# Low rotary score passes of two heads, moved behind all others and cut to 64 rows each

## The reference, cut to what matters

```python
q_rope = apply_rope(q_rope, cos, sin)          # 16 heads, 64 wide
k_rope = apply_rope(k_rope, cos, sin)          # 64 wide, one for all heads
q = concatenate([q_nope, q_rope])              # 128 + 64
k = concatenate([k_nope, k_rope])
s = q @ k.T * scale                            # for each head, causal, blocks of 128 queries
o = softmax(s) @ v
```

## Time and profile before

| | |
|---|---|
| median of 3 runs | 1814.77 us (1813.79 to 1815.86) |
| profiled execution, span from first to last instruction | 1812.8 us |
| profiled execution, own time beside the span | none is given |
| TensorE busy | 1792.2 us, 99%, mean granted clock 0.998 |
| VectorE busy | 1501.2 us, 83% |
| ScalarE busy | 918.5 us, 51% |
| GpSimd busy | 181.3 us, 10% |
| attention, 8 pairs of heads | from 129.6 us, first score matmuls 31.8 us apart |

### The profile page before, as it was taken

The page is one execution under the profiler, slowest core; times in us unless marked ns, Lnnn a source line. Parts: engine busy times, 40 slices in busy tenths (PEclk is TensorE's granted clock), DMA queues, the critical chain, the costliest instruction groups (busy, mean ns, idle before and its releaser), DMA issues.

```text
span 1812.8 us, 28067 instructions
## 1 busy us (share of the span) xinstructions
PE 1792.2 (99%) x10892; PEld 1609.5 (89%) x10892; DVE 1501.2 (83%) x1837; ACT 918.5 (51%) x1163; POOL 181.3 (10%) x100
## 2 busy tenths in 40 slices
PE   9999999999999999999999999999999999999997
PEld 7888989978879999999999999988888888888886
DVE  4167677799989988888888888889888999989986
ACT  5357666544356656655665566543433334333442
POOL 2353323000020000000000000000011111100003
PEclk9999999999999999999999999999999999999999
DMA  6232433598124654565456545778375474754832
GB/s 235 82 105 91 131 119 129 201 360 303 71 106 174 232 209 174 185 214 209 174 184 214 211 174 181 252 299 334 148 281 197 178 286 162 272 202 162 306 123 93
DMA packets 131731, 351.73 MB, mean 194 GB/s; under 512 B 7632, under 2 KB 80208, under 8 KB 113232
## 3 DMA queue, kind: packets, MB, share of 16 engines
q1 hardware_dynamic: 57264, 275.67, 40.7%
q10 hardware_dynamic: 74400, 75.26, 12.6%
HBM read 268.59 MB, written 82.31 MB: 194 GB/s over the span
## 4 chain that ended last, share of the span: by engine, by line
PE 95%; DVE 3%; issue 1%; ACT 1%; DMA 0%; ACTq 0%; DVEq 0%
PE bank L2121 31%; PE bank L2125 31%; PE bank L2126 31%; PE bank L2291 1%; PE bank L2283 0%; PE bank L2281 0%; DVE w_lo L1497 0%; DMA first_raw<-weights 0%; DVE small L1607 0%; DVE up_lo L1703 0%; DVE small L1452 0%; DVE pt_lo L1470 0%; ACT rows L1153 0%; DVE norm_t L1695 0%; DVE rows L1676 0%
## 5 line engine op out<-in xcount | busy, mean ns | idle before, releaser
L2121 PE MATMUL bank<-up_hi,w_hi 128*128 128x256 f32 x1808 | 512.0, 283 | 1.1 <-issue 0.9
L2125 PE MATMUL bank<-up_lo,w_hi 128*128 128x256 f32 x1808 | 511.7, 283 | 0.0
L2126 PE MATMUL bank<-up_hi,w_lo 128*128 128x256 f32 x1808 | 511.6, 283 | 0.0
L2121 PEld LDWEIGHTS bank<-up_hi,w_hi 128*128 128x128 f32 x1808 | 347.1, 192 | 1.8 <-issue 1.6
L2125 PEld LDWEIGHTS bank<-up_lo,w_hi 128*128 128x128 f32 x1808 | 347.1, 192 | 0.0
L2126 PEld LDWEIGHTS bank<-up_hi,w_lo 128*128 128x128 f32 x1808 | 347.1, 192 | 0.0
L1212 ACT ACTIVATE w_hi<-d_b 128x1024 fp32r<-128x1024 f32 x180 | 189.5, 1061 | 299.5 <-PE bank L2126 243.2
L2121 PE MATMUL bank<-w_hi,down_act 128*128 128x512 f32 x864 | 336.6, 390 | 0.0
L2125 PE MATMUL bank<-w_lo,down_act 128*128 128x512 f32 x864 | 336.2, 389 | 0.0
L2126 PE MATMUL bank<-w_hi,down_act 128*128 128x512 f32 x864 | 336.2, 389 | 0.0
L1000 ACT ACTIVATE w_hi<-up_b 128x1024 fp32r<-128x1024 f32 x180 | 186.9, 1054 | 157.9 <-PE bank L2126 126.7
(11 more groups left out here) (214 smaller groups left out, 2931.8 us busy)
## 6 DMA issues: line engine op xcount, KB each, us to landing
up_b<-up_weights SPq DMA_DIRECT2D x128, 512.0 KB, 5.0
d_b<-down_weights SPq DMA_DIRECT2D x64, 1024.0 KB, 5.1
down_act<-acts_kept SPq DMA_DIRECT2D x56, 1024.0 KB, 4.9
acts_kept<-h_hi ACTq DMA_DIRECT2D x32, 896.0 KB, 5.9
acts_kept<-h_lo ACTq DMA_DIRECT2D x32, 896.0 KB, 6.8
raw<-weights SPq DMA_DIRECT2D x46, 512.0 KB, 3.2
o_b<-out_weights SPq DMA_DIRECT2D x16, 1024.0 KB, 7.6
o_act<-o_kept SPq DMA_DIRECT2D x13, 1024.0 KB, 9.3
```

Of the source, the lines that this page charges most:

```text
L2121: first_pass = pe.matmul(out_, a_hi, b_hi, start=start, stop=False, skip_group_check=more)
L2125: pe.matmul(out_, a_hi, b_lo, start=False, stop=False, skip_group_check=more)
L2126: return pe.matmul(out_, a_lo, b_hi, start=False, stop=stop, skip_group_check=more)
```

## The change

The low rotary pass is taken out of `scores` and done for both heads in a new function `score_lows`, called after the scores of both heads. It takes the 64 rows with the high part of the query only, head 0's in rows 0 to 63 and head 1's in rows 64 to 127 (`tile_position` 0 and 64), block by block, the heads alternating. `kr_lo` becomes one tile without zeros. `scored` is now raised twice, by the last two matmuls of `score_lows`. Since block 0 stays open while block 2 of the same bank begins, block 2 no longer starts with the flag that clears.

```diff
-        kr_hi, kr_lo = sb("kr_hi", [P, S], f32r), sb("kr_lo", [P, 2, S], f32r)
-        place[0] += 2 * KB
+        kr_hi, kr_lo = sb("kr_hi", [P, S], f32r), sb("kr_lo", [P, S], f32r)
+        place[0] += 4 * KB
...
-            for h in range(2):
-                last = dve.memset(kr_lo[64 - 64 * h:128 - 64 * h, h, :].bitcast(f32), 0.0)
-            last.then_inc(zeroed, 1)
...
             def key_rope_lo():
                 dve.wait_ge(rope_hi, 1)
-                dve.wait_ge(zeroed, 1)
-                for half, h in zip(halves, range(2)):
-                    last = dve.tensor_tensor(kr_lo[half, h, :], rot[half, :], kr_hi[half, :].bitcast(f32), ALU.subtract)
-                last.then_inc(rope_split, 1)
+                dve.tensor_tensor(kr_lo[:, :], rot[:, :], kr_hi[:, :].bitcast(f32), ALU.subtract).then_inc(rope_split, 1)
...
+            def score_block(h, t):
+                return score_bank(h)[:, SCORE_AT[t]:SCORE_AT[t] + P * (t + 1)]
+
             def scores(pair, h):
...
                 for t in range(TT):
                     q, keys = slice(P * t, P * t + P), slice(0, P * (t + 1))
-                    dst = score_bank(h)[:, SCORE_AT[t]:SCORE_AT[t] + P * (t + 1)]
-                    product(dst, q_hi[:, h, q], q_lo[:, h, q], k_hi[:, h, keys], k_lo[:, h, keys], True, False)
-
-                    pe.matmul(dst, qr[:, h, q], kr_hi[:, keys], start=False, stop=False)
-
-                    last = pe.matmul(dst, qr[:, h, q], kr_lo[:, h, keys], start=False, stop=True)
-                last.then_inc(scored, 1)
+                    product(score_block(h, t), q_hi[:, h, q], q_lo[:, h, q], k_hi[:, h, keys], k_lo[:, h, keys], t != 2, False, t == 2)
+
+                    pe.matmul(score_block(h, t), qr[:, h, q], kr_hi[:, keys], start=False, stop=False,
+                              skip_group_check=t == 2)
+
+            def score_lows():
+                for t in range(TT):
+                    q, keys = slice(P * t, P * t + P), slice(0, P * (t + 1))
+                    for half, h in zip(halves, range(2)):
+                        last = pe.matmul(score_block(h, t), qr[half, h, q], kr_lo[half, keys], start=False, stop=True,
+                                         skip_group_check=t == 2, tile_position=(64 * h, 0))
+                        if t == TT - 1:
+                            last.then_inc(scored, 1)
...
             def attention(pair, ahead):
                 scores(pair, 0)
                 scores(pair, 1)
+                score_lows()
```

More of the change, by code:

```diff
@@ L317, in mla_mlp_program @@
         rope_sined, rope_rotated, rope_hi, rope_split = sem("rope_sined"), sem("rope_rotated"), sem("rope_hi"), sem("rope_split")
-        zeroed = sem("zeroed")
         proj_done, proj_hi, proj_split = sem("proj_done"), sem("proj_hi"), sem("proj_split")
```

## The result

The changed kernel takes 1828.68 us in the median of six runs (1827.77 to 1828.97), the kernel before 1815.66 beside it on the same chips (one of its six runs took 6323.61 us; without it the median is 1815.47). The ratio is 1.0071, 95% interval 1.0061 to 1.0081: about 13 us slower (11 to 15). The forecast was 1828.5, an increase of 13.7.

A forecast was written before the change was run, and what follows sets the result against it. TensorE, busy in 99% of the span, was taken to bound the kernel; seven pairs at +1.67 (11.7) plus 2.0 in the last gave +13.7 us on 1814.77, so 1828.5 us, range 1824.0 to 1833.0.

The forecast's parts named there:

- The room of 0.64 and the chain of VectorE: Before the rotary query projection: q_lo had 0.64 us to spare; VectorE starting at 6.18 finishes it at 13.33.
- the 1.9 I named: Sign to look for: TensorE idle about 1.9 us before the first matmul of every rotary query projection.
- +1.67 a pair: Rotary projection starts at 13.48 instead of 11.81 in seven pairs: -0.37 us for matmuls, +2.04 of new wait.
- Nothing else late, nothing before the loop: No second wait in a pair (second key projection has room 0.9 us); VectorE's 2 us saved before the loop gain nothing.
- The low phase, 0.89: Eight 64-row low passes of a pair take 0.89 us instead of 1.26, paced by weight loads of 0.11.
- the lower end of my bounds at 0.63: Low phase of a pair if both heads' matmuls run wholly side by side: 0.63 us, total 1826.4 us.
- the range at up to 0.35: Cost of the switch to 64 rows: nothing in the sum, up to 0.35 us a pair in the range.
- The last pair, +1.98: Last pair, before its transposes: VectorE starts maxima at 6.18 instead of 4.20, +1.98 us, all on the path.
- The clock: Rival: granted clock falls to 1.2 GHz for the rotary projections after the new stalls, 19 us more, about 1848; chance 4%.
- The rival that gains: Rival: no stall for q_lo, so the array gains 3.0 to 5.0 us (1811.8 to 1809.7); chance 5%.

The follow-up runs named there:

- late_signal: Kernel before, matmuls untouched, with head 0's scores signalled only together with head 1's, behind the last low pass: 1834.66 against 1815.85 us.
- behind_128: Changed kernel's late, alternating place for the low passes, but kept as the old 128-row matmuls against keys with zeros: 1832.53 against 1815.85 us for the kernel before.
- each_head_64: Low passes of 64 rows, but each head does its four behind its own other score matmuls and signals there: 1820.87 against 1815.85 us for the kernel before.
- grouped_64: Changed kernel with head 0's four low passes first, then head 1's four, instead of alternating: 1828.60 against 1815.85 us for the kernel before.
- inplace_64: Kernel before with each low pass at 64 rows, right behind its own block's other matmuls: 1838.79 against 1815.28 us.
- after_fitted_2: Changed kernel, VectorE and ScalarE reordered, last pair's low passes at each head's end, exponentials' table loaded early, weights' high part made later: 1822.90 against 1815.12 us.
- after_reordered: Changed kernel with q_lo before head 1's maxima, queries' high parts before the exponentials, o_lo in two pieces: 1820.24 against 1815.28 us for the kernel before.

## Why the prediction was right

The mechanism came as forecast; that the time came within 0.2 us owes something to luck. The increase was 13.0 us in the medians and 14.4 in the profiled spans against 13.7 forecast, and two errors in the low phase cancelled.

*The room of 0.64 and the chain of VectorE.* Right in each link: start at 6.12 (forecast 6.18), maxima of both heads in 5.08 (5.06), q_lo done at 13.28 (13.33), restart 0.13 (0.15), rotary projection at 13.41 (13.48). late_signal shows the cause by itself; behind_128 and each_head_64 show that it is the place and not the rows. The idle in the records is 1.65 instead of the 1.9 I named: TensorE is free for the rotary projection at 6.01 + 0.12 + 5.46 = 11.59, not at 11.44, since the first matmul behind the 64-row ones takes 0.12 more (236.18 to 236.53 against 0.23).

*+1.67 a pair.* Measured +1.67 in the first and +1.72 in the other six (364.22 - 163.10 = 201.12, a sixth is 33.52).

*Nothing else late, nothing before the loop.* Beside q_lo and the last pair's transposes no wait of TensorE in the pairs grew by more than 0.1 us, and the first pair's scores start at 129.64 us instead of 129.60.

*The low phase, 0.89.* The size was right, 0.92 from where the next matmul would have started (235.26) to 236.18, but its parts were not. I took weight loads one after another at 0.11 as the bound and no price for the switch. The narrow windows show the loads of both heads together and the next two 0.11 later (first lines of windows from 235.3, loads):

```profile
235.34 0.19 PEld L2285 LDWEIGHTS bank<-kr_lo,qr 64*128 64x128 f32 x2 [0.36 <-issue]
...
235.34 0.30 PEld L2285 LDWEIGHTS bank<-kr_lo,qr 64*128 64x128 f32 x4 [0.36 <-issue]
```

So the overlap is whole, the lower end of my bounds at 0.63; grouped_64 adds that it needs no alternation. The Trainium skill (TensorE: Matmul & The Clock Gate, Part 3, Packing small matmuls) says that matmuls on different row groups run concurrently, and the trace agrees: eight take the 0.83 us of four. What the sum had at nothing, and the range at up to 0.35, is the price of the stay. The way into 64 rows and back costs 0.38 to 0.41 us (0.40 in each_head_64, 0.38 in inplace_64, and here 0.92 + 0.12 - 0.63). The Trainium skill (TensorEngine Tiling (Array Packing), Key Properties) says that a change of the tiling mode drains the engine. A price for each stay agrees with that, but the records can't show a drain: the first 64-row matmul starts at 235.35, while the 128-row one before it is recorded from 235.03 for 0.39 us, with a modelled end. Of a possible 0.63 the array gives 0.22 a pair. Two errors of opposite sign met; since the path runs through VectorE, either alone would have moved the forecast by under 4 us.

*The last pair, +1.98.* Measured +1.93 at the transposes. It isn't covered behind them: the last matmul of probabilities by values starts 21.96 after the pair's first score matmul (386.18), in the kernel before 20.04 (372.23).

*The clock.* It did not fall in the profiled run of the changed kernel (1.00 in both windows, mean 0.998 as before). That was luck in part, and 4% was bold. Other kernels had it at 0.50 after the same idle or a shorter one (last section). But no run has the fall that I priced, one in each rotary projection for 19 us.

*The rival that gains* was priced at 3 to 5 us. With the wait removed it gets 0.22 in each of seven pairs, 1.5 us: the array's gain was never large enough to be told from no change.

## What to carry to other kernels

Before moving work behind other work on a full engine, look at who is released by it: the room of the next result (here 0.64 us between q_lo and the matmul that overwrites its bank) decides, not the columns saved. A signal that came halfway through a phase and now comes at its end delays the engine behind it by the half it lay beside (2.74 us here), and what the room doesn't cover is lost (1.7 a pair). Row-tiled matmuls of 64 rows ran two at a time in both orders of issue tried, but group as many as possible into one stay: each stay cost about 0.4 us.

## What I hadn't expected of the hardware

After an idle of 6.46 us (after_fitted_2) TensorE's granted clock was 0.50, the level of 1.2 GHz, and matmuls of 512 columns started 0.43 us apart instead of 0.23. The window:

```profile
339.00:340.00 1.00, 1.00 (x3) 0.73 (x3) 0.93 (x5) 0.97 (x4) 0.00 (x0) 0.50 0.91 301
```

Much shorter idles were followed by the same, and the length alone doesn't decide. In the last pair the changed kernel and after_reordered both idle 2.31 us before the same transposes; the clock stayed at 1.00 in the first and fell in the second. It also fell after 2.29 us in behind_128, and in the first pair of late_signal after 1.77 us (0.50 from 144.9 to 148.2). The window behind the idle in the changed kernel, then the idle and the window in after_reordered:

```profile
377.00:380.00 3.00, 2.63 (x16) 2.02 (x16) 2.96 (x6) 2.80 (x5) 0.00 (x0) 1.00 0.96 391
```

```profile
367.71 1.97 PE L2301 MATMUL bank<-table,probs 128*128 128x128 f32 x10 [2.31 <-DVE probs L1459]
...
368.20:371.60 3.40, 3.40 (x13) 2.93 (x12) 3.36 (x8) 2.50 (x5) 0.00 (x0) 0.50 0.91 358
```

VectorE instructions with operands in SBUF only lost about 2 us when they started within the first 0.4 us of one of GpSimd's subtractions of 2.4 us (3.47 against 1.28, 2.69 against 0.69, 3.95 against 2.02). Who starts first matters: in after_reordered the second piece of o_lo, started 0.29 us ahead of GpSimd, keeps its 1.23 us, and GpSimd's two subtractions take 5.63 us instead of the 4.84 in the kernel before. VectorE instructions that read PSUM did not change. The piece of o_lo, then GpSimd's two:

```profile
251.47 1.23 DVE L1486 TENSOR_TENSOR o_lo<-o_raw,o_hi 128x1024 fp32r<-128x1024 f32 x1
```

```profile
251.76 5.63 POOL L656 TENSOR_TENSOR w_lo<-raw,w_hi 128x1024 fp32r<-128x1024 f32 x2 [6.95 <-ACT w_hi L734]
```
